# Experts' second products with the activations stationary, and work of the next stage drawn into the gate table

## The reference, cut to what matters

```python
PEER_NKEYS = 128; PEER_EXPERTS = PEER_NKEYS * PEER_NKEYS     # 16384, D_MODEL = 1024, 256 tokens
def chunk(args):
    hc, ec, gc = args
    u = expert_u[ec]
    act = jax.nn.gelu(jnp.einsum('td,thkd->thk', hc, u), approximate=False)
    return jnp.einsum('thk,thkd->td', gc * act, expert_v[ec])
...
x = x + gate2 * peer_ffn(h2, peer_wq[l], peer_keys[l], peer_u[l], peer_v[l])
h = rms_norm(x, norm1_g[l]) * (1.0 + scale1) + shift1        # the next layer starts from x
```

## Time and profile before

| | us |
|---|---|
| median of 3 runs | 2645.64 (2645.15 to 2651.74) |
| the profiled execution: its time | 2647.66 |
| its span, first to last instruction | 2645.8 |
| PE matmul busy | 2455.5 (93%) |
| PE weight load busy | 2375.3 (90%) |
| DVE busy | 1784.2 (67%) |
| ACT busy | 1087.5 (41%) |
| mean granted TensorE clock | 0.963 |

### The profile page before, as it was taken

How to read it: one execution, slowest core, us unless ns; L and a number is a source line. 1 busy time by engine, 2 the same in 40 slices (tenths; PEclk the granted TensorE clock), 3 DMA queues, 4 the chain that set the end, 5 groups by cost and what they waited for, 6 DMA issues and landing times. The chain is left out here.

```text
span 2645.8 us, 44334 instructions
## 1 busy us (share of the span) xinstructions
PE 2455.5 (93%) x18280; PEld 2375.3 (90%) x18280; DVE 1784.2 (67%) x2789; ACT 1087.5 (41%) x1584; POOL 192.2 (7%) x141
## 2 busy tenths in 40 slices
PE   5689998999999999979999899999999888788998
PEld 5589897999999999879889899999999877777998
DVE  8879876676666666768977575555555478455665
ACT  4442233444444444444133444444444332344544
POOL 0000274000000000000067000000000000000000
PEclk9889998999999999989999999999999889898999
DMA  9255433786666666424633585555555522342553
GB/s 355 97 212 164 146 108 111 237 301 221 231 229 230 221 230 206 147 81 137 190 98 107 179 296 193 181 183 182 182 182 183 173 89 71 104 152 80 180 187 112
DMA packets 133047, 460.75 MB, mean 174 GB/s; under 512 B 15152, under 2 KB 15408, under 8 KB 132400
## 3 DMA queue, kind: packets, MB, share of 16 engines
q1 hardware_dynamic: 132912, 458.90, 51.3%
HBM read 445.73 MB, written 13.11 MB: 173 GB/s over the span
## 5 line engine op out<-in xcount | busy, mean ns | idle before, releaser
L1392 DVE TENSOR_TENSOR ring_lo<-ring,ring_hi 128x1024 fp32r<-128x1024 f32 x427 | 522.8, 1225 | 369.1 <-ACT ring_hi L1339 369.1
L1339 ACT ACTIVATE ring_hi<-ring 128x1024 fp32r<-128x1024 f32 x427 | 450.2, 1055 | 442.1 <-PE banks L322 278.4
L308 PE MATMUL banks<-normed_hi,ring_hi 128*128 128x256 f32 x2096 | 598.9, 286 | 8.6 <-DVE ring_lo L337 8.5
L320 PE MATMUL banks<-work_lo,ring_hi 128*128 128x256 f32 x2048 | 581.7, 284 | 22.9 <-DVE work_lo L1412 22.9
L310 PE MATMUL banks<-normed_hi,ring_lo 128*128 128x256 f32 x2096 | 593.9, 283 | 0.0
L309 PE MATMUL banks<-normed_lo,ring_hi 128*128 128x256 f32 x2096 | 593.8, 283 | 0.0
L321 PE MATMUL banks<-work_lo,ring_hi 128*128 128x256 f32 x2048 | 581.2, 284 | 0.0
L322 PE MATMUL banks<-work_lo,ring_lo 128*128 128x256 f32 x2048 | 581.1, 284 | 0.0
L320 PEld LDWEIGHTS banks<-work_lo,ring_hi 128*128 128x128 f32 x2048 | 395.0, 193 | 23.7 <-DVE work_lo L1412 23.7
L308 PEld LDWEIGHTS banks<-normed_hi,ring_hi 128*128 128x128 f32 x2096 | 403.2, 192 | 11.0 <-ACT arena L2089 8.7
L309 PEld LDWEIGHTS banks<-normed_lo,ring_hi 128*128 128x128 f32 x2096 | 403.2, 192 | 0.5
(11 more groups left out here) (342 smaller groups left out, 3010.8 us busy)
## 6 DMA issues: line engine op xcount, KB each, us to landing
ring<-wstream SPq DMA_DIRECT2D x716, 512.0 KB, 3.3
arena<-wstream SPq DMA_DIRECT2D x96, 512.0 KB, 5.1
spill<-one_hots SPq DMA_DIRECT2D x44, 256.0 KB, 4.1
pool_and_keys<-spill SPq DMA_DIRECT2D x16, 256.0 KB, 4.0
rstd<-spill SPq DMA_DIRECT2D x14, 256.0 KB, 4.1
routes<-spill SPq DMA_DIRECT2D x14, 256.0 KB, 4.3
residual<-xT SPq DMA_DIRECT2D x1, 1024.0 KB, 7.9
arena<-mixconst SPq DMA_DIRECT2D x2, 512.0 KB, 4.5
```

The lines of the kernel that those rows point to most:

```text
L308: pe.matmul(dst, w_hi[:, o], hi[:, k, :], start=(k == 0), stop=False)
L320: pe.matmul(dst, w_hi[:, o], hi, start=(first and k % 2 == 0), stop=False, skip_group_check=True)
L1339: sc.activation(RING_HI[:, u % HIGHS, :], RING[:, u % SLOTS, :], ACT.Copy)\
L1392: dve.tensor_tensor(RING_LO[:, u % SLOTS, :], RING[:, u % SLOTS, :], RING_HI[:, u % HIGHS, :].bitcast(F32), ALU.subtract).then_inc(S("spli ...
```

## The change

1. `second_product` calls `unit_wide` in place of `unit_spread`: the activation tile of 128 experts x 128 tokens is stationary, and 512 weight columns pass. 2 halves x 2 token tiles x 3 = 12 matmuls a unit. Banks 4 to 7 now hold tokens on the partitions.
2. So at the end ACT copies the four banks to `Y` (in the arena), PE turns them back with 16 transposes, and only then DVE adds them to X. PE's sums wait for the fourth of these additions.
3. In the gate table's block: the first three V units are split (ACT after its last three copies, DVE after its last one-hots); reloads 0 and 1 are issued when the V units begin to stream; the end waits for these and not for the last spill (its semaphore now lives across blocks, and whoever needs it waits there). The slots of `HOT` and `STAGE` are turned so that the freed ones are those the first splits need. One ahead unit (8 chunks) comes before the first group, and the groups' shares shrink accordingly.
4. The experts' block begins with weighting pair 0; ACT waits for both last spills before it writes the fourth V unit's high part.

```diff
+        def unit_wide(pe, u, hi, lo, first, last, done=None):
+            w_hi, w_lo = parts_of(u)
+            for n in range(2):
+                for tt in range(TT):
+                    t, o, dst = slice(tt * P, (tt + 1) * P), slice(n * 512, (n + 1) * 512), PS[:, 4 + 2 * tt + n, :]
+                    pe.matmul(dst, hi[:, t], w_hi[:, o], start=first, stop=False)
+                    pe.matmul(dst, hi[:, t], w_lo[:, o], start=False, stop=False)
+                    mm = pe.matmul(dst, lo[:, t], w_hi[:, o], start=False, stop=last)
+                    if done and n + tt < 2:
+                        mm.then_inc(S(done), 1)
+            return mm
...
-                return 2 * KD * (AHEAD - AHEAD_PICK) * (g + 1) // GROUPS
+                return KD + KD * (2 * (AHEAD - AHEAD_PICK) - 1) * (g + 1) // GROUPS
...
+                        if i == 2 * AHEAD:
+                            for p in range(2):
+                                sp.wait_ge(spilled[p], kept + 16)
+                                if p == 1:
+                                    sp.wait_ge(S("keys_copied"), 8)
+                                sp.dma_start(RAW[p], SPILL[layer, p]).then_inc(S(f"reloaded{p}"), 16)
                     spill(AHEAD - 1)
-                    for q in range(2):
-                        sp.wait_ge(S(f"spilled{q}"), 16 * (AHEAD // 2))
+                    for p in range(2):
+                        sp.wait_ge(S(f"reloaded{p}"), 16)
...
+                    for _ in range(KD):
+                        next(first)
                     for g in range(GROUPS):
...
+                        if g >= GROUPS - PRE:
+                            split_high(act, S_EXP + V0 + g - (GROUPS - PRE), True)
...
+                    highs = N_WQ - PRE
+                    for q in range(PRE):
+                        split_low(v, S_EXP + V0 + q, highs + q)
+                    v.wait("split", highs + PRE)
...
-                    for p in range(3):
-                        reload(p)
+                    reload(2)
...
-                            unit_spread(pe, S_EXP + i + e, E_HI[:, s, o], E_LO[:, s, o], first and e == 0,
-                                        last and e == 1, "spread" if last and e == 1 else None)\
+                            unit_wide(pe, S_EXP + i + e, E_HI[:, s, o], E_LO[:, s, o], first and e == 0,
+                                      last and e == 1, "y_bank" if last and e == 1 else None)\
...
                     for k in range(KD):
+                        if k % 4 == 0:
+                            pe.wait_ge(S("y_copied"), k // 2 + 2)
+                        for tt in range(TT):
+                            mm = pe.transpose(PS[:, k // 2, (k % 2) * T + tt * P:(k % 2) * T + (tt + 1) * P],
+                                              Y[:, tt, k * P:(k + 1) * P], ident)
+                        if k % 2:
+                            mm.then_inc(S("y_turned"), 1)
+                    pe.wait_ge(S("x_done"), 4)
+                    for k in range(KD):
                         sum_chunk(pe, k)
...
                     for p in range(AHEAD - 1):
-                        high(V0 + 2 * p, 0)
-                        high(V0 + 2 * p + 1, 0)
+                        if p == PRE // 2:
+                            for q in range(2):
+                                sc.wait_ge(spilled[q], kept + 16 * (AHEAD // 2))
+                        if 2 * p >= PRE:
+                            high(V0 + 2 * p, 0)
+                        if 2 * p + 1 >= PRE:
+                            high(V0 + 2 * p + 1, 0)
                         e_high(p, p % 2)
...
+                    for n in range(2):
+                        for tt in range(TT):
+                            if n + tt < 2:
+                                act.wait("y_bank", 2 * n + tt + 1)
+                            else:
+                                sc.wait_ge(units_used, S_END)
+                            act.mark(sc.activation(Y[:, tt, n * 512:(n + 1) * 512], PS[:, 4 + 2 * tt + n, :], ACT.Copy),
+                                     "y_copied")
...
-                            if k < KD - 2:
-                                v.wait("spread", k // 2 + 1)
-                            else:
-                                dve.wait_ge(units_used, S_END)
-                        v.mark(dve.scalar_tensor_tensor(X[:, k, :], PS[:, 4 + k // 2, (k % 2) * T:(k % 2 + 1) * T],
+                            v.wait("y_turned", k // 2 + 1)
+                        v.mark(dve.scalar_tensor_tensor(X[:, k, :], PS[:, k // 2, (k % 2) * T:(k % 2 + 1) * T],
```

More of the change, by code:

```diff
@@ L192, in program @@
         CROW_KEPT = nc.dram_tensor("c_row_kept", (P, D), F32, kind="Internal").ap()
-        RAW = [PK[:, 0:512], RS[:, 0:2, :].rearrange("p a t -> p (a t)"), J[:, 0:2, :].rearrange("p a t -> p (a t)")]
+        RAW = [RS[:, 0:2, :].rearrange("p a t -> p (a t)"), PK[:, 0:512], J[:, 0:2, :].rearrange("p a t -> p (a t)")]
         loaded = [ctx.enter_context(nc.semaphore(f"loaded{i}")) for i in range(SLOTS)]
         units_used = ctx.enter_context(nc.semaphore("units_used"))
+        spilled = [ctx.enter_context(nc.semaphore(f"spilled{q}")) for q in range(2)]
         pools = [[ctx.enter_context(nc.semaphore(f"stage{q}_{i}")) for i in range(70)] for q in range(2)]
@@ L1020, in program @@
             HOTS, GROUPS = HIGHS - 1, T // 4
-            hot = HOT[:, 0:HOTS, :].rearrange("p s (m t i) -> p s m t i", m=2, t=4)
+            V0 = 2 * AHEAD
+            slot_of = [(S_EXP + V0 + q) % HIGHS for q in range(HIGHS)]
+            hots = [HOT[:, slot_of[(q - GROUPS) % HOTS], :].rearrange("p (m t i) -> p m t i", m=2, t=4) for q in range(HOTS)]
+            STAGE = HOT[:, slot_of[HIGHS - 1], :].rearrange("p (s c) -> p s c", s=2)
+            kept = 16 * (AHEAD // 2) * layer
             def ahead_by(g):
-                return 2 * KD * (AHEAD - AHEAD_PICK) * (g + 1) // GROUPS
+                return KD + KD * (2 * (AHEAD - AHEAD_PICK) - 1) * (g + 1) // GROUPS
             with nc.Block() as block:
@@ L1102, in _ @@
                         for t in range(4):
-                            mm = pe.matmul(PS[:, g % 4, t * P:(t + 1) * P], hot[:, g % HOTS, 0, t, :],
-                                           hot[:, g % HOTS, 1, t, :], start=True, stop=True)
+                            mm = pe.matmul(PS[:, g % 4, t * P:(t + 1) * P], hots[g % HOTS][:, 0, t, :],
+                                           hots[g % HOTS][:, 1, t, :], start=True, stop=True)
                         mm.then_inc(S("g_made"), 1)
-                        for _ in range(ahead_by(g) - (ahead_by(g - 1) if g else 0)):
+                        for _ in range(ahead_by(g) - (ahead_by(g - 1) if g else KD)):
                             next(first)
@@ L1295, in _, with made_before @@
                 def _(pe):
+                    def made_before(pe, i, r):
+                        if i >= V0 + PRE or i < V0:
+                            pe.wait_ge(S("split"), r * SLOTS + (i + 1 - V0 - PRE))
                     def first_product(i, r, bank):
                         for e in range(2):
-                            pe.wait_ge(S("split"), r * SLOTS + (i + e + 1 - V0))
+                            made_before(pe, i + e, r)
                             unit_product(pe, PS[:, bank, e * T:(e + 1) * T], S_EXP + i + e, H_HI, H_LO)\
@@ L1390, in low @@
                         u = S_EXP + i
-                        dve.wait_ge(S("high"), r * SLOTS + (i + 1 - V0))
+                        dve.wait_ge(S("high"), r * SLOTS + (i + 1 - V0 - PRE))
                         dve.tensor_tensor(RING_LO[:, u % SLOTS, :], RING[:, u % SLOTS, :],
@@ L1436, in _ @@
                     for p in range(AHEAD - 1):
-                        low(V0 + 2 * p, 0)
-                        low(V0 + 2 * p + 1, 0)
+                        if p:
+                            if 2 * p >= PRE:
+                                low(V0 + 2 * p, 0)
+                            low(V0 + 2 * p + 1, 0)
                         weight_ahead(p)
```

17 lines of the change are left out of this document (9 added, 8 removed).

## The result

| | before | after |
|---|---|---|
| median, measured side by side | 2648.69 us | 2591.57 us |
| ratio | | 0.9782 (95%: 0.9767 to 0.9797) |
| span of the profiled execution | 2645.8 us | 2590.5 us |

The change makes the kernel 57 us faster; the forecast was 32 us. First the page's head of after, which answers rows 1: 3040 matmuls fewer, and weight loads busy for 86% of the span and no longer 90%.

A forecast was written before the change was run, and what follows sets the result against it. PE's rate was taken to bound the experts' steps, with two gaps at their edges. The terms -12.3 - 11.5 - 11.5 + 3.2 = -32 us gave 2613.5 us against the median of 2645.6, range 2600 to 2633.

The forecast's parts named there:

- What bounds the kernel: In the experts' steps only PE's own rate counts; PE also waits in two gaps at that stage's edges.
- Step 1, the wide form: Experts' second products: 236 ns a wide matmul against 240 for two narrow ones, 12 us less.
- the two readings under it: Experts' wide matmul: the moving tensor sets the rate, 233.4 ns, or the pair of tensors does, 239 ns.
- The sign of being wrong that I had named: Middle of the experts: the prediction is wrong if the distance between wide matmuls' starts leaves 233 to 240 ns.
- The bound after it: Experts' pairs 14 to 20, where DVE also modulates: some 0.4 us remain at 5.66 us a pair.
- Step 2, the early unit: Gate table's start: one unit moved into the 3.83 us gap, no clock fall expected, 11.5 us less.
- Step 3, table to experts: Gate table to experts: PE starts 5.65 us after the last ahead matmul, not 11.42; 11.5 us less.
- Step 4, the end: Experts' end: copies and transposes delay the sums by 1.6 us a layer, 3.2 us more.
- The slower one (over 246 ns): Experts' wide matmul dearer than two narrow ones, no faster from 246.5 ns; 2663 us at 252 ns; chance 0.09.
- The wide form gains nothing: Experts' second products: 239 to 241 ns a wide matmul, 2626 us; chance 0.20.
- The loads were the bound: Experts' second products: the wide form goes at the f32 passes' 216 ns, 2556 us; chance 0.04.

The follow-up runs named there:

- the two edges that were undone: The changed kernel without the early unit, 2597.7 us; the changed kernel with SP waiting for both last spills again before the gate table's block ends, 2595.7 us.

## Why the prediction was right or wrong

**What bounds the kernel: right.** PE is never idle in the steps of either kernel, and the gain is in PE's rate and the two gaps.

**Step 1, the wide form: the price was wrong, and so were the two readings under it.** The failing step is the sentence that the rate is set either by the moving tensor (233.4 ns) or by the pair of tensors (239 ns). Both take a rate from the cross-attention, whose activations lie elsewhere, and the middle of them, 236 ns, gave 12 us for the experts' stretch, which got shorter by 37.6. The sign of being wrong that I had named came true: the wide distance, 227.8 ns, lies outside 233 to 240. What the runs showed in its place: with the experts' own tensors at their own place it is the width that counts. The same columns in twice as many matmuls go at exactly the old 120.0 ns, whichever operand is stationary.

A third reading was open to me from rows 2 alone. At granted clock 1.00 and a column a cycle 256 columns take 106.7 ns, and 13.3 of the 119.9 are left; if these belong to the matmul and not to its columns, the wide form takes 213.3 + 13.3 = 226.7 ns, and the gain is 13.3 x 3072 = 41 us. That is close to what came, but it would have been right with some luck: at 64 bytes of padding the same reasoning gives 213.3 + 6.7 = 220 ns, and the wide form goes at 230.5. Why the wide form costs 227.8 ns at this placement stays open; the runs show that it depends on where the operands lie, and so does the narrow form's 120.0. I had a warning: 216 ns for 512 columns stood there as a rival with 0.04, and I went from it to 233 without asking what lies between.

The middle of two readings was no estimate either. The cross-attention's 233.4 ns is the 213.3 of its columns and 20 of its own, and with padding of 32 bytes the experts' wide form goes at 233.1. A row of the same form had another price for a reason that the row doesn't show.

The Trainium skill, "TensorE: Matmul & The Clock Gate", section "Back-to-back issue gap", gives N / 2.4 + 2.5 ns as the gap of a single matmul at the higher clock. This agrees with the f32 records (215.7 ns); the fp32r ones show 6.7 to 20 ns in place of 2.5, by placement.

**The bound after it: right, and by less than I said.** In pairs with modulation I left DVE 0.4 us at 5.66 us a pair. The 0.54 us that this rests on the earlier trace rows is the longest wait of its kind; in four of the pairs around it DVE waits 0.26 us there, so 0.2 would have been left. The pair now takes 5.44 us, and DVE's only idle time in it is the 0.70 us for ACT's high part of the pair: nothing is left. PE and DVE end together; from this I take it that a still faster PE would gain nothing in these seven pairs, which no run tried.

**Step 2, the early unit: right.** Gap 0.38 us (forecast 0.4), clock 1.00, 5.3 us a layer for 5.8. Undoing it brings the gap and the low clock back. In the whole time undoing it cost 6 us, not 11, since other stretches changed with it; I had not reckoned with that, and its cause is open.

**Step 3, table to experts: right.** 5.50 us for 5.65, and the fourth V unit's wait for the spill is covered. The experts' first 5.47 us stand at clock 0.50 where it was 4.33 before; I had expected much the same, and the difference stays within the bounds.

**Step 4, the end: right in kind.** +0.6 and +1.7 us for +1.6. The transposes take 1.94 us for 16 (0.12 each, forecast 0.11), and the sums end 6.0 us after the last matmul, in the forecast's 6 to 7.

**The rivals.** The slower one (over 246 ns) did not come about. "The wide form gains nothing" had 0.20 and gave 2626 us, further off than the forecast on the same side. "The loads were the bound" gave 2556, too low by 36 us where the forecast was too high by 22; its cause has something to it, since the narrow form falls from 120.0 to 116.0 ns with a shorter load. The range had the edges' bounds right; it was too high because its lower end took 233.4 ns for the best that the wide form could do, save for the rival at 216.

## What to carry to other kernels

Before a rate per column is compared with another, take the columns' own time at the granted clock away and look at what is left for each instruction: 119.9 - 106.7 = 13.3 ns here. Halving the number of matmuls nearly halved that part at this placement (14.5 ns for 512 columns), but not at the one with 64 bytes of padding (6.7 ns for 256, 17.2 for 512), so a form is to be measured at the place where its operands will lie. Where PE never waits, check the placement of its operands first: 192 bytes of padding gave 53 us, three lines of it against a change with new banks, copies and transposes. Price an edge by following the chain step by step from the last event of the old stage; the three edges priced that way came out within 1.0 us a layer each. And judge a change of a few microseconds in its own stage: the two edges that were undone showed about 5.5 and 2.7 us a layer there, and 6 and 4 us in the whole.

## What the runs showed of the hardware

- fp32r matmuls back to back at the change's placement and clock 1.00: 120.0 ns for 256 columns, with activations or weights stationary alike, and 227.8 for 512 with the activations stationary. In a mix of the two, 384 and 128 columns take 286 ns together; two of three distances are 175 and 111.5 ns.
- The same narrow form goes at 113.4 or 120.0 ns by a shift of 64 bytes of the tile that it reads eight times over, with the ring's high part moved by 128 bytes besides; the FFN's, whose tile lies 64 bytes off in every kernel, goes at 113.5 to 114.3 in the mean of its whole stage in every kernel, whether the ring's high part has moved or not. For `H`, whose eight chunks are read in turn, 64 bytes give 117.7 and 32 give 117.1. The wide form has its best value, 227.8, where the narrow one has its worst, and 230.5 at 64 bytes, 233.1 at 32. A shift of the work tile and the ring's high part by 128 bytes against the ring's low part gives 232.2. I have no rule that gives these numbers; whether `H` can be placed so that the first products go at 113.4 as well, which would be 26 us more, was not tried.
